# Two of eight remainder subtractions per phase moved from VectorE to GpSimd in the expert stage of a streaming encoder kernel

## The chip, the cores and the metric

One core of a Trainium2 chip. The time is the device time of one launch in microseconds, as the median of several runs.

## The reference

One layer of a streaming encoder runs on 512 prompt tokens and 128 sample tokens: a convolution branch and a gated delta-rule branch, merged by gates, then PEER expert retrieval, then a final norm. The change lies in the retrieval. Cut to what matters:

```python
def peer(xn, w_q, sub_keys, u, v):          # 16384 experts, 8 heads, top 16 of each
    ...                                     # idx, gate: (tokens, 8, 16)
    def block(args):
        xb, ib, gb = args
        hid = jnp.einsum('pd,phkd->phk', xb, u[ib])    # u, v: (16384, 2048)
        act = jax.nn.gelu(hid) * gb
        return jnp.einsum('phk,phkd->pd', act, v[ib])
```

## The kernel before

All is float32. There are five tiles of 128 tokens, and the expert stage treats them in two ways at once.

**Dense, tiles 0 to 2 (384 tokens).** TensorE multiplies the tokens with all 16384 rows of the first table `u`, GELU and a scattered gate follow, and the result is multiplied with the second table `v`. A float32 product is made of three passes with values cut in two: the high part (`xhi`, `whi`, `vhi`, `ahi`) and the remainder (`xlo`, `wlo`/`ulo`, `vlo`, `alo`). ScalarE makes each high part of a table's unit by a copy that rounds (`high`, `high_v`), and VectorE makes the remainder by a subtraction, raw minus high (`low` for the first table, L2857; `low_v` for the second, L2877). A unit is 128 x 1024 values, 512 KB.

**Gathered, tiles 3 and 4 (256 tokens).** Each token fetches only the rows of its 128 chosen experts. GpSimd asks for them by indirect DMAs of 128 rows of 2048 values (L2998): `u_rows` into two buffers `urow`, `v_rows` into two buffers `vrow`. VectorE takes a dot product with each row of `u` (`gather_dot`, L2899) and adds each row of `v` with its weight into the sum (`gather_add`, L2919). A request waits until the operation that used the row two numbers earlier is done, so that the two buffers alternate.

The stage runs in phases `c` = 1 to 32 with eight steps `j` = 0 to 7. Phases 2 to 31 are the full ones, 30 of them. The order on each engine is written out by hand. In a step of a full phase:

- TensorE: 24 matmuls of the first table (L2565, L2570), then it waits for the step's remainder `vlo`, then 18 matmuls of the second table (L2610 to L2612).
- ScalarE: `high` for the next step, `gelu_tile` in even steps, `high_v` for this step, `high_a` in odd steps from 3 on.
- VectorE: `low` for the next step, in even steps `gate` (L2867), `gather_dot`, `low_v` for this step, in odd steps from 3 on `low_a` (L2872), then `add_pair` (even, L2885, reads PSUM) or `add_third` (odd, L2893, reads PSUM), then `gather_add`.
- GpSimd: `u_rows`, then `v_rows`, and nothing else.
- SyncE and ScalarE's queue load the raw units.

The number of dots per step is one, with one exception that `dots` sets: in the phases 5, 10, 15, 20, 25 and 30 step 4 has two (I call these extra phases, the other 24 quiet ones):

```python
more = (c - 1) // 5 + (1 if c % 5 == 0 and j > NU // 2 else 0)
return min(FIRST_DOTS[NU] + (c - 2) * NU + j + more, GATHERS)
```

Of the kernel before, what the change touches and what calls it, by code (L numbers as in the profile page):

```python
# [85 lines left out]
def build(nc, x_prompt, x_sample, consts, params, conv_prefix, dconv_prefix, state_in, w_ba, w_first, w_units,  # L86
          keys, ffn_g, final_g, peer_u, peer_v, u_units, v_units,
          y_prompt, y_sample, conv_new_p, dconv_new_p, state_new_p, conv_new_s, dconv_new_s, state_new_s):
    with ExitStack() as ctx:
# [2228 lines left out]
        def sem2(name):  # L2318
            return ctx.enter_context(nc.semaphore(name))
# [86 lines left out]
        gt_ld = sem2("gt_ld")  # L2406
        hi_done, lo_done, unit_free, v_mm = (sem2(n) for n in ("hi_done", "lo_done", "unit_free", "v_mm"))
        gelu_done, a_done, v_add = (sem2(n) for n in ("gelu_done", "a_done", "v_add"))
        a_mul, a_hi, vhi_done, vlo_done = (sem2(n) for n in ("a_mul", "a_hi", "vhi_done", "vlo_done"))
        ggelu, gcoef, u_used, v_used = (sem2(n) for n in ("ggelu", "gcoef", "u_used", "v_used"))  # L2410
        u_ld = [sem2(f"u_ld{i}") for i in range(2)]
        v_ld = [sem2(f"v_ld{i}") for i in range(2)]
# [35 lines left out]
        def row_sums(c, j):  # L2448

            return 0 if c == 1 else (c - 2) * GRP + j if c < CHUNKS else TAIL + 2 * j  # L2450
        assert dots(CHUNKS - 1, NU) == dots(CHUNKS, 0) == GATHERS and row_sums(CHUNKS, NU) == GATHERS

        def phases(phase):

# [77 lines left out]
        def _(pe):  # L2532
# [50 lines left out]
            def phase(c, par, has_u):  # L2583
                for j in range(NU):
                    if has_u:
                        first_table(c * NU + j, j % 2, c * ET + j // 2, j // 2 % 2, lows=None if c == 1 else ulo[j % URING])
                    vh4, vl4 = (a.rearrange("p (e x) -> p e x", e=2) for a in (vhi[:, j % 2, :], vlo[j % VRING]))
                    v4 = vraw[j % VRING].rearrange("p (e x) -> p e x", e=2)
                    b, half = j // 2, j % 2
                    if has_u:  # L2590
                        pe.wait_ge(vlo_done, c * NU + (j + 1 - NU))
                    else:
                        pe.wait_ge(vn_ld[j % VRING], c * VLOADS + (16 * (j // VRING) + 16 - VLOADS))
                    for t in range(DT):
                        out = v_sum(b, t)
                        if half == 0 and t != 1:
                            pe.wait_ge(v_add, (c - 1) * NU + 2 * b + 1 + t // 2)
                        tok = slice(t * P, (t + 1) * P)
                        for q in range(2):
                            e = 2 * half + q  # L2600
                            first, last = half == 0 and q == 0, half == 1 and q == 1
                            if not has_u:
                                if b == 0 and t == 0:
                                    pe.wait_ge(a_hi, c * ET + (e + 1 - ET))
                                mmi = pe.matmul(out, aplain[1 - par][:, e, tok], v4[:, q, :], start=first, stop=last)
                                continue
                            if b == 0 and t == 0:
                                pe.wait_ge(a_done, c * ET + (e + 3 - ET))
                            a_h, a_l = ahi[1 - par][:, e, tok], alo[1 - par][e][:, tok]
                            pe.matmul(out, a_h, vh4[:, q, :], start=first, stop=False)  # L2610
                            pe.matmul(out, a_h, vl4[:, q, :], start=False, stop=False)  # L2611
                            mmi = pe.matmul(out, a_l, vh4[:, q, :], start=False, stop=last)  # L2612
                        if t:
                            mmi.then_inc(v_mm, 1)
# [136 lines left out]
        def _(v):  # L2751
# [177 lines left out]
            def phase(c, par, has_u):  # L2929
                first = is_first(c)  # L2930
                for j in range(NU):
                    if not has_u and j == 0:
                        v.wait_ge(v_used, CHUNKS // GT * GRP + 2)
                        v.sem_inc(f_ready, 1)
                    if not has_u and j == NU - 1:
                        v.wait_ge(f_gain, 16)
                        result(0)
                    if first:
                        low_v(j, j % 2, j % VRING)
                    if has_u and not (j == NU - 1 and is_last(c)):  # L2940
                        if first and j < NU - 1:
                            low_pre(NU + j + 1, (NU + j + 1) % PRE, (j + 1) % 2)
                        else:
                            low(c * NU + (j + 1), (j + 1) % 2, (j + 1) % URING)
                    if j == 0 and not first:
                        gate(c * ET - 1, ET - 1, 1 - par, c * 16 - 32)
                    if j == 0 and not first:
                        gather_coef(c - 2)
                    if j == NU // 2 and not has_u:
                        gather_coef(c - 1)  # L2950
                    if j and j % 2 == 0 and has_u:
                        e = j // 2 - 1
                        if e == 0:
                            wait_count(v, "dve", v_mm, c * KD + (4 - KD))
                        gate(c * ET + e, e, par, c * 16 - 16)
                    for n in range(dots(c, j), dots(c, j + 1)):
                        gather_dot(n)
                    if has_u and not first:
                        low_v(c * NU + (j - NU), j % 2, j % VRING)
                    if j == 0 and not first and has_u:  # L2960
                        low_a(c * ET - 1, ET - 1, 1 - par)
                    if j % 2 and j >= 3 and has_u:
                        e = (j - 3) // 2
                        if not is_last(c):
                            low_a(c * ET + e, e, par)
                    if first and j == 2:
                        v.wait_ge(f_ld, 16)
                    if j >= 2:
                        (add_third if j % 2 else add_pair)(c, j // 2 - 1)
                    elif not first:  # L2970
                        (add_third if j % 2 else add_pair)(c - 1, NU // 2 - 1)
                    if not has_u and j == NU - 1:
                        add_pair(c, NU // 2 - 1)
                        v.wait_ge(v_add, CHUNKS * NU + 3)
                        v.sem_inc(f_ready, 2)
                        add_third(c, NU // 2 - 1)
                        v.wait_ge(v_add, CHUNKS * NU + 4)
                        v.sem_inc(f_ready, 1)
                    for n in range(row_sums(c, j), row_sums(c, j + 1)):
                        gather_add(n)  # L2980
                if first:
                    v.wait_ge(x1g_ld, 16)
# [7 lines left out]
        @block2.gpsimd  # L2990
        def _(pool):
            pool.iota(iota_i2, pattern=[[1, NK]], base=0, channel_multiplier=0).then_inc(iota_ready, 1)
            pool.wait_ge(iota_ready, 1)
            pool.tensor_copy(iota_k[:], iota_i2).then_inc(iota_ready, 1)

            def rows(dst, table, n, ld):

                pool.indirect_dma_start(out=dst, out_offset=None, in_=table,  # L2998
                                        in_offset=bass.IndirectOffsetOnAxis(ap=gidx_all[:, n:n + 1], axis=0)).then_inc(ld, 16)

            def u_rows(n):

                if n == 0:
                    pool.wait_ge(oh_done, NQ)
                    pool.wait_ge(oh_key, NQ)
                elif n == 1:
                    pool.wait_ge(a_mul, ET)
                    pool.wait_ge(g_out[1], 16 * (NGG // 2))
                else:
                    pool.wait_ge(u_used, n + 1)  # L3010
                rows(urow[n % 2], peer_u, n, u_ld[n % 2])

            def v_rows(n):

                if n < TAIL + 2:
                    pool.wait_ge(v_used, n + 1)
                elif n < TAIL + 4:
                    pool.wait_ge(u_used, GATHERS + 2)
                else:
                    pool.wait_ge(v_used, n - 1)  # L3020
                if n < TAIL:
                    rows(vrow[n % 2], peer_v, n, v_ld[n % 2])
                else:
                    rows(tail_row[(n - TAIL) % 4], peer_v, n, tail_ld[(n - TAIL) % 4])

            def phase(c, par, has_u):
                for j in range(NU):
                    for n in range(dots(c, j), dots(c, j + 1)):
                        u_rows(n)
                    for n in range(row_sums(c, j), row_sums(c, j + 1)):  # L3030
                        v_rows(n)
            phases(phase)


# [93 lines left out]
```

## Time and profile before

| | |
|---|---|
| median of 3 runs | 4575.81 us (4572.33 to 4582.88) |
| the profiled execution | 4578.06 us, its span 4576.4 us, mean TensorE clock 0.983 |
| busy in the span | PE 97%, PEld 90%, DVE 75%, ACT 29%, POOL 29% |
| DVE in the second half of the slices | 9 tenths or more nearly throughout |
| DMA in the same slices | 9 tenths, 340 to 406 GB/s |
| L2899 (dots), DVE | 256, 2287 ns each, 585.1 us |
| L2919 (weighted adds), DVE | 256, 2348 ns each, 601.2 us |
| L2877 (`low_v`), DVE | 248, median 1222 ns |
| L2998 (row requests), POOL | 512, 1679 and 1519 ns each |

PE is TensorE's matmuls, PEld its weight loads, DVE VectorE, ACT ScalarE, POOL GpSimd. A share of the span is a mean over stages; the expert stage is the stretch from about 2410 to 4510 us.

### The profile page before, as it was taken

How to read it: one execution, taken by the hardware profiler on the slowest of the kernel's cores; microseconds unless marked ns; L12 is line 12 of the kernel's file. 1: busy time of each engine (PE TensorE's matmuls, PEld its weight loads, DVE VectorE, ACT ScalarE, POOL GpSimd, SP SyncE). 2: the span in 40 equal slices, each digit the busy share in tenths (PEclk: the TensorE clock that was granted, in tenths of full speed). 3: DMA queues.
4: the chain of work that ended last, by engine and by line, in shares of the span. 5: the costliest groups of instructions: out<-in, count | busy, mean ns of one | idle time of the engine just before them, and what ended most of it. 6: DMA issues, size and time to landing. Idle time of an engine off the chain costs nothing.

```text
span 4576.4 us, 67251 instructions
## 1 busy us (share of the span) xinstructions
PE 4426.4 (97%) x26165; PEld 4130.3 (90%) x26165; DVE 3443.6 (75%) x4196; ACT 1342.5 (29%) x1810; POOL 1348.8 (29%) x808
## 2 busy tenths in 40 slices
PE   7999999999999999999698999999999999999997
PEld 7999999999999998889687999989989989999995
DVE  4788884444443331058896999999999999999998
ACT  3323333222221211132282222222222222222222
POOL 0111123122222333323102343333344333343342
PEclk8999999999999999999899999999999999999999
DMA  3222223212224434231179999999999999999998
GB/s 114 88 85 88 84 91 100 75 61 75 79 84 159 136 120 156 87 124 65 58 222 357 391 387 406 389 380 392 388 386 396 394 374 393 389 391 396 394 390 340
DMA packets 255373, 1085.11 MB, mean 237 GB/s; under 512 B 23680, under 2 KB 72192, under 8 KB 181632
## 3 DMA queue, kind: packets, MB, share of 16 engines
q0 software_dynamic: 74752, 538.99, 30.1%
q1 hardware_dynamic: 140032, 400.12, 24.5%
q10 hardware_dynamic: 40320, 142.10, 8.0%
q8 instruction: 207, 3.39, 0.3%
q14 instruction: 62, 0.51, 0.0%
HBM read 1016.24 MB, written 64.88 MB: 236 GB/s over the span
## 4 chain that ended last, share of the span: by engine, by line
PE 44%; DVE 3%; DMA 2%; issue 1%; SPq 0%; ACT 0%; POOL 0%; DVEq 0%; ACTq 0%
PE ps L2565 14%; PE ps L2570 7%; PE ps L2610 7%; PE ps L2611 7%; PE ps L2612 7%; PE ps L2549 1%; DMA work<-in_peer_u,sel 1%; DMA work<-in_peer_v,sel 1%; DMA keep<-in_u_units 0%; DVE work L2899 0%; DVE work L2800 0%; DVE keep L2919 0%; SPq L2502 0%; DVE workr L2877 0%; DVE work L2802 0%
## 5 line engine op out<-in xcount | busy, mean ns | idle before, releaser
L487 PE MATMUL ps<-xhi,hi 128*128 128x320 f32 x2560 | 769.8, 314 | 16.0 <-ACTq L771 9.4
L487 PE MATMUL ps<-xlo,hi 128*128 128x320 f32 x2560 | 757.6, 309 | 0.0
L2565 PE MATMUL ps<-xhi,whi 128*128 128x384 f32 x2048 | 688.0, 336 | 0.0
L2565 PE MATMUL ps<-xlo,whi 128*128 128x384 f32 x2048 | 687.2, 336 | 0.0
L2998 POOL DMA_INDIRECT work<-in_peer_u,sel x256 | 429.9, 1679 | 799.9 <-DVE hid L2899 628.8
L2610 PE MATMUL ps<-vhi,ahi 128*128 128x512 f32 x1488 | 589.2, 396 | 22.9 <-DVE workr L2877 22.6
L2919 DVE SCALAR_TENSOR_TENSOR keep<-work,act_w,keep 128x2048 f32<-128x2048 f32 x256 | 601.2, 2348 | 6.4 <-DMA work<-in_peer_v,sel 5.8
L2899 DVE CUSTOM_DVE_ANT_0 work<-work,keep 128x2048 f32<-128x2048 f32 x256 | 585.1, 2287 | 19.4 <-DMA work<-in_peer_u,sel 18.1
L2611 PE MATMUL ps<-workr,ahi 128*128 128x512 f32 x1488 | 588.9, 396 | 0.0
L2998 POOL DMA_INDIRECT work<-in_peer_v,sel x256 | 388.8, 1519 | 671.0 <-DVE keep L2919 663.3
L2612 PE MATMUL ps<-vhi,alo 128*128 128x512 f32 x1308 | 516.2, 395 | 0.0
L487 PEld LDWEIGHTS ps<-xhi,hi 128*128 128x128 f32 x2560 | 481.7, 188 | 20.3 <-issue 11.6
L487 PEld LDWEIGHTS ps<-xlo,hi 128*128 128x128 f32 x2560 | 481.8, 188 | 2.2 <-issue 2.2
L487 PE MATMUL ps<-xhi,lo 128*128 128x320 f32 x2560 | 435.9, 311 | 0.0
L2565 PEld LDWEIGHTS ps<-xhi,whi 128*128 128x128 f32 x2048 | 384.6, 188 | 10.6
L2565 PEld LDWEIGHTS ps<-xlo,whi 128*128 128x128 f32 x2048 | 384.5, 188 | 10.1
L487 PEld LDWEIGHTS ps<-xhi,lo 128*128 128x128 f32 x2560 | 388.6, 188 | 1.4 <-issue 1.4
L1419 POOL TENSOR_TENSOR lo<-keep,hi 128x1024 fp32r<-128x1024 f32 x80 | 199.8, 2498 | 643.5 <-ACT hi L730 636.5
L2610 PEld LDWEIGHTS ps<-vhi,ahi 128*128 128x128 f32 x1488 | 281.5, 189 | 82.5 <-DVE workr L2877 27.1
L2676 ACT ACTIVATE whi<-work 128x1024 fp32r<-128x1024 f32 x120 | 127.4, 1061 | 723.6 <-PE ps L2570 723.6
L2676 ACT ACTIVATE whi<-wraw 128x1024 fp32r<-128x1024 f32 x120 | 127.4, 1061 | 694.0 <-PE ps L2570 687.7
L2611 PEld LDWEIGHTS ps<-workr,ahi 128*128 128x128 f32 x1488 | 281.3, 189 | 54.8
(349 smaller groups left out, 7806.2 us busy)
## 6 DMA issues: line engine op xcount, KB each, us to landing
work<-in_v_units ACTq DMA_DIRECT2D x256, 512.0 KB
keep<-in_w_first SPq DMA_DIRECT2D x160, 512.0 KB, 3.6
work<-in_u_units SPq DMA_DIRECT2D x120, 512.0 KB
wraw<-in_u_units SPq DMA_DIRECT2D x120, 512.0 KB
keep<-in_w_units SPq DMA_DIRECT2D x32, 1024.0 KB, 4.9
gates_dram<-work SPq DMA_DIRECT2D x8, 3072.0 KB, 11.8
gbuf<-gates_dram SPq DMA_DIRECT2D x30, 768.0 KB
arena<-in_w_units SPq DMA_DIRECT2D x32, 512.0 KB, 4.1
```

The lines of the kernel that those rows point to most:

```text
L487: m = pe.matmul(out[:, o:o + HT], w[:, k, :], x[:, 8 * kh + k, c], start=kh == 0 and i == 0, stop=kh == 1 and i == 23)
L1419: pool.tensor_tensor(lo_w(n), raw_w(n), hi_w(n).bitcast(F32), ALU.subtract).then_inc(lo_done, 1)
L2549: m = pe.matmul(ps[2 + r][:, b * P:(b + 1) * P], oneh[r][0][:, b, :], oneh[r][1][:, b, :], start=True, stop=True)
L2565: pe.matmul(out, h3[:, k, :], (xlo if m % 2 else xhi)[:, 8 * half + k, :], start=half == 0 and m == 0, stop=False)
L2570: mmi = pe.matmul(out, l3[:, k, :], xhi[:, 8 * half + k, :], start=False, stop=half == 1 and k == 7)
L2610: pe.matmul(out, a_h, vh4[:, q, :], start=first, stop=False)
L2611: pe.matmul(out, a_h, vl4[:, q, :], start=False, stop=False)
L2612: mmi = pe.matmul(out, a_l, vh4[:, q, :], start=False, stop=last)
L2676: act.activation(whi[:, r, :], uraw[slot], ACT.Copy).then_inc(hi_done, 1)
L2899: v.tensor_tensor_reduce(out=row, in0=row, in1=xg[:, n // SLOTS, :], scale=1.0, scalar=0.0, op0=ALU.mult, op1=ALU.add, accum_out=hid[:, h: ...
L2919: v.scalar_tensor_tensor(x1g[:, t, :], row, act_w2[:, j:j + 1], x1g[:, t, :], ALU.mult, ALU.add).then_inc(v_used, 1)
L2998: pool.indirect_dma_start(out=dst, out_offset=None, in_=table, in_offset=bass.IndirectOffsetOnAxis(ap=gidx_all[:, n:n + 1], axis=0)).then_ ...
```

## The change

In phases 2 to 31 the remainders of steps 2 and 5 are no longer made by VectorE. GpSimd makes them with the same subtraction, behind the row requests of the following step (3 and 6). It waits for ScalarE's high part and signals on a new semaphore `vlo_shared`; TensorE waits on that one in steps 2 and 5, and the count of VectorE's own remainders, `vector_lows`, is six a phase instead of eight. Phases 1 and 32 are as before. Nothing else changes; the subtraction gives the same values.

```diff
+        SHARED = (2, 5)
+
+        def vector_lows(c, j):
+
+            if c == 1:
+                return j + 1
+            return NU + (c - 2) * (NU - len(SHARED)) + j + 1 - sum(s <= j for s in SHARED)
...
                     if has_u:
-                        pe.wait_ge(vlo_done, c * NU + (j + 1 - NU))
+                        if c > 1 and j in SHARED:
+                            pe.wait_ge(vlo_shared, (c - 2) * len(SHARED) + SHARED.index(j) + 1)
+                        else:
+                            pe.wait_ge(vlo_done, vector_lows(c, j))
...
-                    if has_u and not first:
+                    if has_u and not first and j not in SHARED:
                         low_v(c * NU + (j - NU), j % 2, j % VRING)
...
+            def shared_low(n, r, slot):
+
+                pool.wait_ge(vhi_done, n + 1)
+                pool.tensor_tensor(vlo[slot], vraw[slot], vhi[:, r, :].bitcast(F32), ALU.subtract).then_inc(vlo_shared, 1)
...
                     for n in range(row_sums(c, j), row_sums(c, j + 1)):
                         v_rows(n)
+                    if has_u and c > 1 and j - 1 in SHARED:
+                        shared_low(c * NU + (j - 1 - NU), (j - 1) % 2, (j - 1) % VRING)
```

On VectorE, in step 5 of a full phase, before (ISA rows are the dot and the reading of its sum; L2877 is `low_v`, L2872 `low_a`, L2893 `add_third`, L2919 `gather_add`):

```order
L2857 TENSOR_TENSOR wlo<-wraw,whi 128x1024
L2899 ISA work,hid<-work,keep 128x2048
L2899 ISA hid 128x1
L2877 TENSOR_TENSOR workr<-work,vhi 128x1024
L2872 TENSOR_TENSOR alo0<-hbuf,ahi 128x384
L2893 TENSOR_TENSOR work<-work,ps3 128x512
L2919 SCALAR_TENSOR_TENSOR keep<-work,act_w2,keep 128x2048
```

The same step in the changed kernel, where line numbers are 11 higher:

```order
L2868 TENSOR_TENSOR wlo<-wraw,whi 128x1024
L2910 ISA work,hid<-work,keep 128x2048
L2910 ISA hid 128x1
L2883 TENSOR_TENSOR alo0<-hbuf,ahi 128x384
L2904 TENSOR_TENSOR work<-work,ps3 128x512
L2930 SCALAR_TENSOR_TENSOR keep<-work,act_w2,keep 128x2048
```

The subtraction between the dot and `low_a` is gone; step 2 loses it in the same way, between the dot and `add_pair`. On GpSimd, in the changed kernel, from the row requests of step 3 of a full phase to those of step 7:

```order
L3009 DMA work<-in_peer_u,sel 128x2048
L3009 DMA work<-in_peer_v,sel 128x2048
L3027 TENSOR_TENSOR workr<-work,vhi 128x1024
L3009 DMA work<-in_peer_u,sel 128x2048
L3009 DMA work<-in_peer_v,sel 128x2048
L3009 DMA work<-in_peer_u,sel 128x2048
L3009 DMA work<-in_peer_v,sel 128x2048
L3009 DMA work<-in_peer_u,sel 128x2048
L3009 DMA work<-in_peer_v,sel 128x2048
L3027 TENSOR_TENSOR workr<-work,vhi 128x1024
L3009 DMA work<-in_peer_u,sel 128x2048
L3009 DMA work<-in_peer_v,sel 128x2048
```

Before, this engine had the requests alone; now the subtraction of step 2 stands ahead of the requests of step 4, and that of step 5 ahead of those of step 7.

## Rows read from the trace of the kernel before

**Rows 1.** Windows: busy us of each engine (x instructions), granted clock, DMA, GB/s.

```profile
3500.00:3600.00 100.00, 100.00 (x505) 90.52 (x504) 97.81 (x86) 28.64 (x36) 37.14 (x24) 1.00 1.00 393
...
3070.00:3080.00 10.00, 6.97 (x29) 5.89 (x28) 7.26 (x7) 2.38 (x3) 1.94 (x3) 0.83 1.02 409
...
3750.00:3760.00 10.00, 10.00 (x39) 8.66 (x38) 10.00 (x9) 0.00 (x0) 3.55 (x3) 0.73 0.97 369
```

**Rows 2.** Waits of PE from 2500 to 4500 us: total, times, longest.

```profile
PE ps L2610 <- DVE workr L2877: 7.3, 7, 3.0
```

**Rows 3.** Timeline of DVE, step 2 of phase 17: start, us, what.

```profile
3515.48 2.29 DVE L2899 CUSTOM_DVE_ANT_0 work<-work,keep 128x2048 f32<-128x2048 f32 x1
...
3517.69 1.22 DVE L2877 TENSOR_TENSOR workr<-work,vhi 128x1024 fp32r<-128x1024 f32 x1
3518.83 1.21 DVE L2885 TENSOR_TENSOR work<-work,ps 128x1024 f32<-128x1024 f32 x1
3519.96 2.35 DVE L2919 SCALAR_TENSOR_TENSOR keep<-work,act_w,keep 128x2048 f32<-128x2048 f32 x1
```

**Rows 4.** Timeline of DVE, step 5 of phase 17.

```profile
3540.09 2.28 DVE L2899 CUSTOM_DVE_ANT_0 work<-work,keep 128x2048 f32<-128x2048 f32 x1
```

**Rows 5.** Timeline of POOL in the same phase.

```profile
3513.92 1.99 POOL L2998 DMA_INDIRECT work<-in_peer_v,sel  x1 [2.32 <-DVE keep L2919]
3518.04 1.68 POOL L2998 DMA_INDIRECT work<-in_peer_u,sel  x1 [2.13 <-DVE hid L2899]
...
3539.29 1.69 POOL L2998 DMA_INDIRECT work<-in_peer_v,sel  x1 [2.86 <-DVE keep L2919]
```

**Rows 6.** Timeline of PE: first second-table matmul of steps 2 and 5.

```profile
3520.88 0.39 PE L2610 MATMUL ps<-vhi,ahi 128*128 128x512 f32 x1
...
3545.96 0.39 PE L2610 MATMUL ps<-vhi,ahi 128*128 128x512 f32 x1
```

**Rows 7.** Earlier stages, timeline: DVE and POOL where they overlap.

```profile
810.45 2.40 POOL L1419 TENSOR_TENSOR lo<-keep,hi 128x1024 fp32r<-128x1024 f32 x1 [10.13 <-ACT hi L730]
...
811.99 1.21 DVE L1289 TENSOR_TENSOR arena<-arena,ps 128x1024 f32<-128x1024 f32 x1
...
1466.12 1.22 DVE L1348 TENSOR_TENSOR arena<-arena,smalld 128x1024 f32<-128x1024 f32 x1
...
1466.38 3.19 POOL L1419 TENSOR_TENSOR lo<-keep,hi 128x1024 fp32r<-128x1024 f32 x1 [9.25 <-ACT hi L730]
...
817.71 2.42 POOL L1419 TENSOR_TENSOR lo<-keep,hi 128x1024 fp32r<-128x1024 f32 x1 [4.86 <-ACT hi L730]
...
817.79 2.88 DVE L1302 TENSOR_TENSOR arena<-cst,keep 128x512 f32<-128x512 f32 x1
```

**Rows 8.** Lines of the source: count, ns min/median/max, first and last start.

```profile
L1302 DVE TENSOR_TENSOR arena<-cst,keep x10: 678/685/2889, 817.8 to 1351.3; 128x512 f32<-128x512 f32 x10
...
L1227 DVE SCALAR_TENSOR_TENSOR arena<-arena,par x232: 1117/1134/3284, 141.1 to 708.1; 128x880 f32<-128x880 f32 x116
```

**Rows 9.** Timeline of phase 10, steps 5 and 6 (DVE, POOL, PE).

```profile
3072.74 2.29 DVE L2899 CUSTOM_DVE_ANT_0 work<-work,keep 128x2048 f32<-128x2048 f32 x1 [3.63 <-DMA work<-in_peer_u,sel]
...
3081.03 2.29 DVE L2899 CUSTOM_DVE_ANT_0 work<-work,keep 128x2048 f32<-128x2048 f32 x1
...
3069.10 0.94 POOL L2998 DMA_INDIRECT work<-in_peer_v,sel  x1 [0.30 <-issue]
...
3076.24 0.80 PE L2610 MATMUL ps<-vhi,ahi 128*128 128x512 f32 x1 [3.03 <-DVE workr L2877]
...
3086.21 0.39 PE L2610 MATMUL ps<-vhi,ahi 128*128 128x512 f32 x1
```

**Rows 10.** Timeline of phase 5, step 5 (DVE, PE).

```profile
2737.42 1.23 DVE L2877 TENSOR_TENSOR workr<-work,vhi 128x1024 fp32r<-128x1024 f32 x1
...
2739.32 0.39 PE L2610 MATMUL ps<-vhi,ahi 128*128 128x512 f32 x1
```

**Rows 11.** Chain that ended last, 3055 to 3090 us: start, us, what.

```profile
3061.51 11.21 DMA work<-in_peer_u,sel
```

More of the change, by code:

```diff
@@ L2408, in build @@
         gelu_done, a_done, v_add = (sem2(n) for n in ("gelu_done", "a_done", "v_add"))
-        a_mul, a_hi, vhi_done, vlo_done = (sem2(n) for n in ("a_mul", "a_hi", "vhi_done", "vlo_done"))
+        a_mul, a_hi, vhi_done, vlo_done, vlo_shared = (sem2(n) for n in ("a_mul", "a_hi", "vhi_done", "vlo_done", "vlo_shared"))
         ggelu, gcoef, u_used, v_used = (sem2(n) for n in ("ggelu", "gcoef", "u_used", "v_used"))
```

## Prediction

> **What bounds the kernel now.** I read the windows first. In a quiet stretch of the expert stage PE is busy for 100.00 of 100 us at the full clock, DVE for 97.81, POOL for 37.14, and the DMA share is 1.00 [rows 1]. So TensorE sets the pace there, VectorE has 2.19% left, and the DMA queues have next to nothing left. The reader is to see three engines at their limit at once: work taken off VectorE is worth only what TensorE waits for it. The list of waits gives that: from 2500 to 4500 us TensorE waits 7.3 us in all for `low_v`, seven times, at most 3.0 us [rows 2]. The timelines show where. In a quiet phase `low_v` is ready well ahead: in step 2 it ends at 3517.69 + 1.22 = 3518.91 and TensorE comes at 3520.88, in step 5 it ends at 3543.52 (the dot's start 3540.09, the 2.21 from a dot's start to the next operation's, and 1.22) and TensorE comes at 3545.96 [rows 3, 4, 6]. The gaps are 1.97 and 2.44 us. The 7.3 us lie in the extra phases, most of them in phases 10 and 20. In phase 10 the dot of step 5 waits 3.63 us for its row, then `low_v` follows, and TensorE waits 3.03 us [rows 9]. TensorE's clock falls after that wait: the window 3070 to 3080 has a granted clock of 0.83 (between the levels 2.4 and 1.2 GHz), and after the like wait of phase 20 the window 3750 to 3760 has 0.73 [rows 1]. Those two windows cost 10 x 0.17 = 1.7 and 10 x 0.27 = 2.7 us more.
>
> The profiled execution took 4578.06 us, 2.25 above the median of 4575.81, with 1.7 of it outside its span. The terms below are differences and go onto either.
>
> **VectorE's account, quiet phase.** Removed: two subtractions. From the start of one to that of the next operation it is 3518.83 - 3517.69 = 1.14 us [rows 3], so 2.28 us a phase. Added on GpSimd: two subtractions of the same form as L1419, 2.42 us where it runs at once [rows 7], 4.9 us a phase on an engine that is 37% busy. If they were free for the others, VectorE would gain 2.28 us a phase.
>
> They are not free. Where GpSimd's subtraction and a VectorE operation that reads two tiles of SBUF meet, one waits for the other. At 1466.12 VectorE was first: its 1.22 us are not lengthened, and GpSimd's operation took 3.19. At 817.71 GpSimd was first: VectorE's L1302 took 2.88 us [rows 7] against a median of 0.685, 2.20 more, and L1227 goes from a median of 1.134 to 3.284, 2.15 more [rows 8]. An operation that reads one tile of SBUF and one of PSUM is not touched: L1289 takes 1.21 us at 811.99, inside POOL's subtraction of 810.45 to 812.85 [rows 7]. The Trainium skill, "SBUF — State Buffer", section "Who interferes with whom", has this as a rule: the shared pair of ports goes to whoever issues first, for the whole instruction, the other fully blocks, and a VectorE instruction with two SBUF inputs contends with GpSimd's reads. The trace agrees.
>
> *Step 2.* GpSimd comes to the subtraction after the request of 3513.92, which ended at 3515.91; with about 0.3 us of issue that is 3516.2, inside the dot that runs 3515.48 to 3517.77 [rows 3, 5]. It is granted at the dot's end and VectorE is locked out for 2.15 us from 3517.69, until 3519.84. `add_pair` reads PSUM and runs 3517.69 to 3518.83 beside it. `gather_add` then starts at 3519.84 instead of 3519.96 [rows 3]. Net: -0.12 us.
>
> *Step 5.* The request of 3539.29 ends at 3540.98, the subtraction is asked for at 3541.3, inside the dot of 3540.09 to 3542.37 [rows 4, 5]. What follows the dot is `low_a`, with two SBUF inputs: it is blocked for 2.15 us from 3542.30, where 1.14 were saved. Net: +1.01 us.
>
> So VectorE's load rises by 0.89 us a phase. It has 2.19% of 66.7 us (a step is (3545.96 - 3520.88) / 3 = 8.36 us [rows 6], a phase 66.7) = 1.46 left, and keeps 0.57. Over five phases, with the extra dot (3517.69 - 3515.48 = 2.21 us), 7.3 - 2.2 = 5.1 us were free, and 0.6 remain. That is just enough, and the mechanism decides at a load of 5.1 / 5 = 1.02 us a phase.
>
> **TensorE's waits, quiet phases.** GpSimd's result comes about 2.3 us after the dot's end: 3520.05 in step 2, TensorE at 3520.88; 3544.65 in step 5, TensorE at 3545.96 [rows 3, 4, 6]. The slack shrinks to 0.8 and 1.3 us, no wait. Cost 0. The cover that hides it is TensorE's own work; if GpSimd took 0.8 us longer, each step 2 would cost.
>
> **The row requests behind.** The request of 3518.04 now stands behind the subtraction (3520.3). A request is itself held by a running two-input VectorE operation: that of 3518.04 ends 0.8 us after `low_v`'s end of 3518.91 [rows 3, 5]. Now it meets `gather_add` (until 3522.2) and ends near 3523.0 instead of 3519.72, 3.3 us later. The dot that uses its row comes two steps on, 16.7 - 2.2 = 14.5 us after the old issue; the slow landing shown took 11.21 us [rows 11]. Margin 3.3, delay 3.3: mostly covered, in phases behind an extra one not. I put 1 us in all, bounds 0 and 6.
>
> **Extra phases 10 and 20.** GpSimd reaches the subtraction of step 5 after the request of 3069.10 + 0.94, at 3070.3, while VectorE stands idle until 3072.74 [rows 9]. It is done by 3072.8, before TensorE is ready at 3076.24 - 3.03 = 3073.21. That wait goes. Step 6 of TensorE would then be ready at 3081.5, but its `low_v` follows a dot that can start only 1.14 us earlier than 3081.03 [rows 9]; it ends at 3079.9 + 2.2 + 1.2 = 3083.4. So a wait of 1.9 us is late next, and TensorE starts step 6 at 3083.4 instead of 3086.21: -2.8 us, or -1.1 if the clock falls again for 1.7. I take -2 for each: -4.
>
> **Extra phases 5, 15, 25, 30.** In phase 5 `low_v` was released by the dot at 2737.42 and TensorE came at 2739.32 [rows 10]. Granted at the dot's end (2737.50), GpSimd delivers at 2739.8: a new wait of 0.5. Four times: +2.
>
> **Recovery.** After an extra phase VectorE is late by up to its 2.2 us dot and now catches up by 0.57 a phase instead of 1.46. In step 2 of the five phases behind one GpSimd's result is 1.1 us later than `low_v` was. I put 0.5 for each, +2.5, bounds 0 and 5.6.
>
> **Sum.** 1 - 4 + 2 + 2.5 = +1.5, rounded to +2: 4578 on the median (4580 in the profiled execution's terms). About 0.2%, 9.2 us, is what a measurement here can tell from no change. With the bounds of the terms (-1.1 to -2.8 for each of phases 10 and 20) the sum runs from -4 to +12.
>
> **Rivals.**
> 1. *Slower: VectorE becomes the bound.* If GpSimd comes to step 2's subtraction before the dot (it was 0.7 us behind its start, 3516.2 against 3515.48), the dot is blocked whole, 2.2 - 1.14 = 1.06 us instead of -0.12. With step 5 that is 2.1 us a phase against 1.46 free: 0.66 x 30 = 20 us, and the six extra dots are no longer hidden, 13 us, less the 7.3 us of waits that they already cause: +26, 4602. The break-even load is 1.02 us and I forecast 0.89, so that 0.15 us more in each GpSimd subtraction already costs (0.30 - 0.13) x 30 = 5 us. For it: that narrow margin, VectorE's 97.81%, DMA at 1.00. Against: the request before it is itself held by the subtraction `low`, which keeps it behind the dot's start. Chance 0.34. The Trainium skill, "Perfetto Trace Analysis", section "Optimizing Scalar/DVE Operations", says that moving work between VectorE and GpSimd might not help, since they share a read port; here that would take the form of this rival.
> 2. *Faster: the waits of TensorE go and nothing comes back.* At most the 7.3 us with the clock's 1.7 + 2.7, 12 us: 4564. For it: in phases 10 and 20 the subtraction falls into idle time. Against: [rows 7, 8]. Chance 0.08.
>
> **Chances and range.** The forecast, within 4567 to 4585, has 0.58; slower by over 0.2% 0.34, faster 0.08. The range of eight in ten reaches from 4570 to rival 1's 4602. The likeliest case's own range is 4570 to 4588.
>
> **What the profile after would show.** The subtraction on POOL 60 times, 3.8 us each in step 2 and 3.3 in step 5, since it waits inside for the dot. `low_a` with a maximum near 2.7 us instead of 0.55, in the 30 steps 5; `gather_add` in step 2 near 3.4 us instead of 2.35. `low_v` 188 times. DVE near 98.9 to 99% in the quiet window, PE still at 100. The 3.03 us wait of phase 10 gone, with one of about 2 us in its step 6. PE waiting for POOL in steps 5 of the extra phases. Wrong would make it: dots that are lengthened to 4.4 us in step 2 (rival 1), VectorE operations with two SBUF inputs that keep their length beside GpSimd's (rival 2), or TensorE waiting in the quiet phases.

## The result and the profile after

The changed kernel takes 4610.71 us (median of 4 runs, 4607.92 to 4615.74) against 4574.07 us of the kernel before, measured beside it (4570.01 to 4582.88). The ratio is 1.008, interval 1.0067 to 1.0093. It is 36.6 us slower, and outside the range of the prediction. The profiled execution took 4607.92 us with a span of 4606.3, against 4578.06 and 4576.4 before: 29.9 us more. In all readings of the profile after, line numbers are 11 higher than before: the dot is L2910, `low_v` L2888, `low_a` L2883, `gather_add` L2930, and GpSimd's subtraction L3027.

From the page: busy time, the chain that ended last, and the group of the dot (busy us, mean ns of one, idle before it and what ended most of that).

```profile
PE 4439.5 (96%) x26165; PEld 4128.5 (90%) x26165; DVE 3509.0 (76%) x4136; ACT 1342.6 (29%) x1810; POOL 1496.6 (32%) x868
...
DVE 33%; issue 12%; DMA 3%; PE 3%; SPq 0%; ACT 0%; POOL 0%; DVEq 0%; ACTq 0%
...
L2910 DVE CUSTOM_DVE_ANT_0 work<-work,keep 128x2048 f32<-128x2048 f32 x256 | 675.2, 2639 | 19.0 <-DMA work<-in_peer_u,sel 17.9
```

VectorE lost 60 subtractions, yet its busy time rose. A dot takes 2639 ns in the mean where it took 2287. The chain that ended last holds 33% of VectorE and 3% of TensorE; in the kernel before it held 3% and 44%.

The windows after, first the quiet one that answers to [rows 1], then phases 3 to 30 whole (from TensorE's first second-table matmul of phase 3 to that of phase 31):

```profile
3500.00:3600.00 100.00, 99.76 (x500) 89.63 (x500) 99.93 (x83) 29.26 (x38) 46.49 (x27) 1.00 0.99 389
...
2562.30:4474.14 1911.84, 1886.53 (x9410) 1692.58 (x9410) 1900.49 (x1553) 544.43 (x700) 880.67 (x510) 1.00 0.98 385
```

The same 28 phases of the kernel before:

```profile
2563.75:4444.79 1881.04, 1873.50 (x9410) 1694.73 (x9409) 1836.70 (x1608) 544.39 (x700) 737.15 (x454) 1.00 0.99 390
```

VectorE's work grew from 1836.70 to 1900.49 us: 63.8 us, or 2.28 a phase. Its idle time fell from 44.3 to 11.4 us, so 33.0 us of the growth went into idle time, and the other 30.8 came onto the stage, which is 1911.84 - 1881.04 = 30.8 us longer, the 29.9 of the span within a microsecond. Such a split comes out for any engine, since busy and idle time add up to the window. What makes VectorE the bound is how little of it is left idle. The same windows phase by phase, over the 22 quiet ones among these 28: VectorE was idle for 1.37 us in the mean before and for 0.03 to 0.04 us in each of them after; a quiet phase grew by 0.81 us, 17.9 in all. The six extra phases together grew by 12.9, from 414.4 to 427.3. The granted clock of both windows is 1.00, so the loss is not the clock's.

Where the growth sits, the timelines show. Step 2 of phase 17, POOL and then DVE:

```profile
3528.12 1.69 POOL L3009 DMA_INDIRECT work<-in_peer_v,sel  x1 [2.32 <-DVE keep L2930]
3529.83 2.41 POOL L3027 TENSOR_TENSOR workr<-work,vhi 128x1024 fp32r<-128x1024 f32 x1
```

```profile
3529.38 5.02 DVE L2910 CUSTOM_DVE_ANT_0 work<-work,keep 128x2048 f32<-128x2048 f32 x1
...
3534.33 1.21 DVE L2896 TENSOR_TENSOR work<-work,ps 128x1024 f32<-128x1024 f32 x1
```

GpSimd's subtraction begins 0.02 us after its request ends and takes the 2.41 us of an unhindered one. The dot is recorded as starting 0.45 us ahead of it, and still it takes 5.02 us instead of 2.29 [rows 3]: it is the dot that waited, 2.73 us. This is so in 29 of the 30 steps 2; in the first of them GpSimd starts 0.23 us ahead of the dot, which takes 4.48. Step 5 of the same phase:

```profile
3555.93 3.61 POOL L3027 TENSOR_TENSOR workr<-work,vhi 128x1024 fp32r<-128x1024 f32 x1
```

```profile
3555.02 2.28 DVE L2910 CUSTOM_DVE_ANT_0 work<-work,keep 128x2048 f32<-128x2048 f32 x1
...
3557.23 2.73 DVE L2883 TENSOR_TENSOR alo<-hbuf,ahi 128x384 fp32r<-128x384 f32 x1
```

Here the dot starts 0.91 us ahead and keeps its 2.28; GpSimd waits inside (3.61), and `low_a` then takes 2.73 instead of 0.55. By the single operations a full phase has 2.73 - 1.14 = +1.59 us in step 2 and 2.18 - 1.14 = +1.04 in step 5, 2.63 together. The windows' 2.28 is less mainly because a `gather_add` with idle time behind it counts 2.35 us, and one that the next operation follows at once 2.26 up to that operation's start. In phase 17 four had idle time behind them before and none has after: 0.36 us, which leaves 2.27. In the steps 5 of the extra phases one dot (3.4 to 4.5 us) bears the conflict.

TensorE's waits from 2500 to 4530 us (total, times, longest), which were 7.3 us for one line before [rows 2]:

```profile
PEld ps L2621 <- DVE workr L2888: 29.4, 39, 2.4
PE ps L2621 <- DVE workr L2888: 18.1, 10, 2.1
PEld ps L2621 <- POOL workr L3027: 14.0, 22, 0.8
...
PE ps L2621 <- POOL workr L3027: 6.9, 21, 0.4
```

PE and PEld wait beside each other, so the rows don't add up. There are many short waits, most for VectorE's `low_v`, some for GpSimd's result: VectorE is late everywhere. A quiet phase takes 67.2 to 67.8 us instead of 66.45 or 66.88, by TensorE's first second-table matmuls; the extra phases 5, 15, 25 and 30 take 71.2, 71.2, 71.1 and 72.5 instead of 67.3, 68.2, 67.3 and 66.9; phases 10 and 20 got shorter, 70.6 and 70.8 instead of 71.8 and 72.9.

### The profile page after: what moved, and what is told of

It is laid out like the page before. It is cut to its first block, busy times and chain, and to the rows that moved or that the text cites. A ratio compares the mean times of both kernels' runs of the same rounds, so it can differ in the third digit from the quotient of the medians.

```text
span 4606.3 us, 67251 instructions
## 1 busy us (share of the span) xinstructions
PE 4439.5 (96%) x26165; PEld 4128.5 (90%) x26165; DVE 3509.0 (76%) x4136; ACT 1342.6 (29%) x1810; POOL 1496.6 (32%) x868
## 4 chain that ended last, share of the span: by engine, by line
DVE 33%; issue 12%; DMA 3%; PE 3%; SPq 0%; ACT 0%; POOL 0%; DVEq 0%; ACTq 0%
DVE work L2910 12%; DVE keep L2930 7%; DVE workr L2888 4%; DVE work L2896 3%; DVE alo L2883 2%; DMA work<-in_peer_u,sel 2%; DVE work L2904 2%; PE ps L2557 1%; DVE hbuf L2878 1%; DMA work<-in_peer_v,sel 1%; DVE wlo L2868 1%; PE ps L2573 1%; DVE workr L2868 1%; DMA keep<-in_u_units 0%; DVE work L2811 0%
## 5 line engine op out<-in xcount | busy, mean ns | idle before, releaser
L2910 DVE CUSTOM_DVE_ANT_0 work<-work,keep 128x2048 f32<-128x2048 f32 x256 | 675.2, 2639 | 19.0 <-DMA work<-in_peer_u,sel 17.9
L3009 POOL DMA_INDIRECT work<-in_peer_v,sel x256 | 414.9, 1621 | 652.8 <-DVE keep L2930 646.7
L3009 POOL DMA_INDIRECT work<-in_peer_u,sel x256 | 384.2, 1501 | 693.9 <-DVE hid L2910 519.4
L2930 DVE SCALAR_TENSOR_TENSOR keep<-work,act_w,keep 128x2048 f32<-128x2048 f32 x256 | 600.8, 2347 | 8.1 <-DMA work<-in_peer_v,sel 7.4
```

What stands on the lines that cost most here:

```text
L2910: v.tensor_tensor_reduce(out=row, in0=row, in1=xg[:, n // SLOTS, :], scale=1.0, scalar=0.0, op0=ALU.mult, op1=ALU.add, accum_out=hid[:, h: ...
L2930: v.scalar_tensor_tensor(x1g[:, t, :], row, act_w2[:, j:j + 1], x1g[:, t, :], ALU.mult, ALU.add).then_inc(v_used, 1)
```

## The experiments

The names in the expectations: A is the theory that VectorE's load is the cause and that in step 2 the dot is blocked whole; B puts the loss elsewhere (TensorE waiting for GpSimd's late results, or requests standing behind the subtractions). Each edit is against the changed kernel. Where a memset is added the dot is L2911 and the subtraction L3030 to L3032.

**Each half alone.**

```diff
-        SHARED = (2, 5)
+        SHARED = (2,)
```

> GpSimd makes the remainder of step 2 alone; step 5 is VectorE's again. Theory A (load): in the changed kernel's trace the dot of step 2 takes 5.01 us instead of 2.28, so VectorE loses 2.73 and saves 1.14, +1.59 us a phase, against 1.02 us that it has free on the mean of five phases. 0.57 x 30 = 17 us more than before: 4591 (4586 to 4596). Theory B (late results): TensorE waits for GpSimd's result and for late rows, and that happens in step 5 (the waits for POOL lie there); without it the time is before's within 4 us, 4570 to 4578. The dot is long in 30 steps 2 by either theory.

Measured: 4581.16 us (4578.10 to 4584.15) against 4576.27, ratio 1.0009, interval 1.0 to 1.0019.

```diff
-        SHARED = (2, 5)
+        SHARED = (5,)
```

> GpSimd makes the remainder of step 5 alone. Theory A: the dot keeps its 2.28 us, the alo subtraction behind it takes 2.73 instead of 0.55, so VectorE loses 2.18 and saves 1.14, +1.04 us a phase against 1.02 free on the mean: between 0 and +6 us, 4574 to 4580. Theory B: most of the 36 us stay, above 4595.

Measured: 4579.02 us (4572.19 to 4583.02), ratio 1.0001, interval 0.9991 to 1.0011.

In the first, the dots' maximum is 5.021 us, as in the changed kernel; in the second `low_a` reaches 2.750. In the window 3500 to 3600 VectorE is busy for 99.90 us with step 2 alone and for 98.85 with step 5 alone, and TensorE stays at 100.00 in both.

Neither half costs anything like half of 36.6 us: step 2 alone adds 4.9 us, step 5 alone at most 5. That is how a threshold looks, and step 5 alone speaks for A and against B, whose cost for it was about 20 us or more. But step 2 alone lies in neither range: A, with a break-even load of 1.02 us a phase, expected 4586 to 4596, B 4570 to 4578. The trace shows where the threshold lies. By the windows of its 22 quiet phases VectorE's busy time is 1.38 us a phase above that of the kernel before, which had 1.37 us idle; 0.05 us are left idle, and the phase is 66.72 us long instead of 66.67. So step 2 alone fills VectorE just to the brim.

**The two remainders by nobody.** In phases 2 to 31 the remainders of steps 2 and 5 are left out, and the second pass of their products takes the high part again, so the output is not the reference's. This is the upper bound of what any helper could give.

```diff
-                            pe.wait_ge(vlo_shared, (c - 2) * len(SHARED) + SHARED.index(j) + 1)
+                            pe.wait_ge(vhi_done, c * NU + (j + 1 - NU))
+                            vl4 = vh4
...
-                    if has_u and c > 1 and j - 1 in SHARED:
-                        shared_low(c * NU + (j - 1 - NU), (j - 1) % 2, (j - 1) % VRING)
```

> The two remainders are left out of the computation: nobody makes them, and the pass over the remainder in steps 2 and 5 uses the high part again, so TensorE's work is the same. This is what the removal from VectorE alone is worth. Both theories: VectorE's load falls by 2.28 us a phase, the waits of TensorE of 7.3 us and the clock's loss of up to 4.4 us behind them go for the most part: -5 to -11 us, 4563 to 4569. If it were -20 or more, TensorE would not be the bound of the stage before.

Measured: 4572.02 us (4569.21 to 4579.46) against 4576.27, ratio 0.9984, interval 0.9974 to 0.9994. That is 4 us faster than before by the medians and 7 by the ratio, and above the 4563 to 4569 expected. VectorE falls to 94.62 of 100 us. All there was to win is about 0.1 to 0.2%.

**Who comes first in step 2.** Two memsets of 240 columns on GpSimd, each waited for, stand ahead of step 2's subtraction.

```diff
+        pause, paused = sb2("pause", [P, 240]), sem2("paused")
...
+                if r == 0:
+                    for k in range(2):
+                        pool.memset(pause[:], 0.0).then_inc(paused, 1)
+                        pool.wait_ge(paused, (n // NU) * 2 + k - 1)
                 pool.wait_ge(vhi_done, n + 1)
```

> As the changed kernel, but in step 2 GpSimd first does two small memsets one after the other (about 0.3 us each), so that its subtraction is asked for about 1 us after the dot's start instead of 0.45. Theory A with order of arrival as the cause of the long dot: the dot of step 2 keeps 2.28 us, GpSimd's subtraction takes 3.4 to 3.8 us, the weighted add of step 2 takes about 3.4; VectorE's load is +0.9 instead of +2.63 us a phase, and the time is 4576 to 4586. Theory A with the dot losing whatever the order: dot 5.0 us, 4610. Theory B: the result comes later than now, so 4610 or more.

Measured: 4581.01 us (4577.04 to 4584.80), ratio 1.001, interval 1.0001 to 1.002. GpSimd does more, yet the kernel is some 30 us faster than the changed one. In 29 of the 30 steps 2 the dot starts 1.18 us ahead of the subtraction and keeps 2.28, and `gather_add` takes 3.35. The first case is of another kind; POOL and DVE in step 2 of phase 2:

```profile
2513.74 4.05 POOL L3032 TENSOR_TENSOR workr<-work,vhi 128x1024 fp32r<-128x1024 f32 x1
```

```profile
2513.26 2.29 DVE L2911 CUSTOM_DVE_ANT_0 work<-work,keep 128x2048 f32<-128x2048 f32 x1
```

The dot is only 0.48 us ahead and wins. In the changed kernel it was 0.45 ahead and lost. And in step 5 of phase 15 of this same kernel, where GpSimd comes straight from a request, it is 0.59 ahead and loses:

```profile
3413.50 2.41 POOL L3032 TENSOR_TENSOR workr<-work,vhi 128x1024 fp32r<-128x1024 f32 x1
```

```profile
3412.91 5.16 DVE L2911 CUSTOM_DVE_ANT_0 work<-work,keep 128x2048 f32<-128x2048 f32 x1 [0.24 <-DMA work<-in_peer_u,sel]
```

So no single bound on the recorded lead decides. The next pair tests why: C says that a subtraction right behind a request takes the shared reads before its recorded start, D that any small delay on GpSimd is enough.

**A one-column memset without and with a wait.** `pause` has one column here. First without:

```diff
+                if r == 0:
+                    pool.memset(pause[:], 0.0).then_inc(paused, 1)
                 pool.wait_ge(vhi_done, n + 1)
```

> As the changed kernel, with one memset of a single column on GpSimd ahead of the subtraction of step 2, and no wait between them. Theory C (early claim): the subtraction claims the shared read interface while the row request ahead of it is still being finished, so before its recorded start; that is how the dot loses though it is recorded 0.45 us earlier. A memset that waits for nobody lets the claim through: the dot of step 2 stays near 5.0 us, load +2.6 us a phase, 4600 to 4612. Theory D (a dot claims late, some 0.5 us after its recorded start, since it is a custom operation): a delay of 0.1 to 0.2 us is enough, the dot keeps 2.28 and the time is 4577 to 4586.

Measured: 4610.52 us (4609.04 to 4611.17) against 4574.64, ratio 1.0077, interval 1.0061 to 1.0094. Then the same memset, waited for:

```diff
+                if r == 0:
+                    pool.memset(pause[:], 0.0).then_inc(paused, 1)
+                    pool.wait_ge(paused, n // NU)
                 pool.wait_ge(vhi_done, n + 1)
```

> The same with a wait for that memset ahead of the subtraction, so that the subtraction can't begin before everything ahead of it on GpSimd is complete. Theory C: the dot keeps its 2.28 us, the subtraction takes 3.7 to 4.1 us, 4577 to 4586. Theory D: as e5, the dot 2.28 us as well if the delay reaches 0.5 us after the dot's start, otherwise 5.0. C and D are told apart by e5 together with this one: they differ in C and are alike in D.

Measured: 4580.36 us (4578.99 to 4586.50), ratio 1.0016, interval 1.0007 to 1.0026. The one wait is worth 30 us. The timelines of a step 2, without the wait:

```profile
3532.83 0.11 POOL L3029 MEMSET pause<- 128x1 f32 x1
3532.88 2.41 POOL L3030 TENSOR_TENSOR workr<-work,vhi 128x1024 fp32r<-128x1024 f32 x1
```

```profile
3532.39 5.06 DVE L2911 CUSTOM_DVE_ANT_0 work<-work,keep 128x2048 f32<-128x2048 f32 x1
```

and with it:

```profile
3517.27 0.11 POOL L3029 MEMSET pause<- 128x1 f32 x1
3517.46 3.91 POOL L3031 TENSOR_TENSOR workr<-work,vhi 128x1024 fp32r<-128x1024 f32 x1
```

```profile
3516.83 2.28 DVE L2911 CUSTOM_DVE_ANT_0 work<-work,keep 128x2048 f32<-128x2048 f32 x1
...
3520.17 3.35 DVE L2931 SCALAR_TENSOR_TENSOR keep<-work,act_w,keep 128x2048 f32<-128x2048 f32 x1
```

Without the wait the dot is 0.49 us ahead (0.47 to 0.49 in nearly all steps) and loses. With a wait it won at a lead of 0.48 in the run before this, and wins here at 0.62. In all the traces together a dot beside a subtraction that comes straight from a request loses at recorded leads up to 0.60 us and wins from 0.69 on, with none in between. At equal leads the wait decides, so recorded starts alone don't. C holds, D falls.

The length of a beaten dot says the same. A dot longer than 2.5 us occurs 118 times in the traces of all runs, each time beside a subtraction, and it ends 2.15 to 2.16 us after the subtraction's end, whether it is recorded as starting 0.60 us ahead of the subtraction or 1.5 us behind. What it is recorded as running before GpSimd's start brings it nothing.

The second timeline is step 2 as the prediction had it: the dot keeps its length, and GpSimd's turn falls beside `add_pair`. `gather_add` is then 1.01 us longer where 1.14 was saved, -0.13 us net; the prediction said -0.12. And the kernel takes 4580, where it said 4578. GpSimd makes the same two remainders a phase here and ends that of step 2 4.54 us after the dot's start, where the changed kernel takes 2.86; so late results, theory B, aren't the cause.

The Trainium skill, "GPSIMD Engine Reference", section "Instruction dispatch", warns that GpSimd's cores do not run in lockstep: each goes on to the next instruction once its own share of the one before is done. That would make such an early claim possible. The trace shows the claim and what removes it, not the single cores, so this reading is not shown.

**Is it the shared reads?** GpSimd writes zeros instead of the difference, so it reads nothing. The remainders of these two steps are then zero: this kernel leaves their part of the product out.

```diff
-                pool.tensor_tensor(vlo[slot], vraw[slot], vhi[:, r, :].bitcast(F32), ALU.subtract).then_inc(vlo_shared, 1)
+                pool.memset(vlo[slot].bitcast(F32), 0.0).then_inc(vlo_shared, 1)
```

> GpSimd writes zeros in place of each of the two remainders, at the same places and with the same waits: the subtraction is left out of the computation, and GpSimd reads nothing from SBUF there. If it is the shared read interface that blocks VectorE, the dot of step 2 keeps 2.28 us and the alo subtraction of step 5 0.55, and the time is that of e3 within 4 us, 4567 to 4575. If any work of GpSimd there does it (its write, or its late requests), both stay lengthened and the time stays above 4590.

Measured: 4574.85 us (4568.63 to 4580.80), ratio 0.9998, interval 0.9988 to 1.0007. Its lines of the source for the dot and `low_a` (count, ns min/median/max):

```profile
L2910 DVE CUSTOM_DVE_ANT_0 work<-work,keep x256: 2281/2285/2361, 2429.4 to 4490.2; 128x2048 f32<-128x2048 f32 x128
```

```profile
L2883 DVE TENSOR_TENSOR alo<-hbuf,ahi x105: 547/553/559, 2449.1 to 4437.8; 128x384 fp32r<-128x384 f32 x105
```

Same order, same waits, same writes into the same buffer: no dot is above 2.36 us and no `low_a` above 0.56. The memset starts 0.43 us behind the dot of step 2, where the subtraction started 0.45 behind, and runs beside it for all of its 0.97 us without either getting longer. So the blocking of the dot goes with the two operands that GpSimd reads. In step 5 the memset is done before the dot ends, and `low_a` doesn't meet it: there the run shows that the loss goes with the subtraction, and not whether a write of the same length would block `low_a`.

**Another step.**

```diff
-        SHARED = (2, 5)
+        SHARED = (1, 5)
```

> GpSimd makes the remainders of steps 1 and 5 instead of 2 and 5. Step 1 has no gate ahead of its dot, so the dot should win there as in step 5; behind it stands the third add, 0.60 us and reading PSUM, and then the weighted add, which is held: 2.18 - 0.60 - 1.14 = +0.44. With step 5's +1.04 the load grows by 1.48 us a phase. The mean phase of the kernel before is 67.2 us with its stalls, VectorE's work 65.2 and 0.44 for the extra dots, so 1.57 are free. Theory A: 4574 to 4582, and 25 to 35 us faster than the changed kernel with the same number of subtractions moved. If the number of subtractions on GpSimd is what counts, 4605 or more.

Measured: 4584.90 us (4581.99 to 4589.73), ratio 1.0021, interval 1.0011 to 1.0031. The same number of remainders, 25.8 us faster than the changed kernel: the rival by which the mere number moved decides (4605 or more) falls. The remainder of step 1 falls beside VectorE's step 1, an odd one with no `gate` ahead of the dot, so the dot starts 0.92 us before the subtraction and keeps its 2.28, and `gather_add` takes 3.88. The load is 3.88 - 2.35 - 1.14 = +0.39 and +1.04, 1.43 a phase; by the windows of the quiet phases 1.34, just under the 1.37 free. It came out 3 us above what was expected; with so little free, single phases (the one behind each extra phase takes 67.1 to 67.8 instead of 66.45 or 66.88) already pay.

**Only where VectorE stands idle.** The remainder of step 5 in phases 10 and 20 goes to GpSimd, nothing else.

```diff
+        def is_shared(c, j):
+
+            return c in (10, 20) and j == 5
...
```

> GpSimd makes one remainder only, that of step 5 in phases 10 and 20, where VectorE stood idle for 3.63 us (phase 10) waiting for rows; everywhere else as before. Theory (what a phase gains or loses is set by VectorE's free time in it, and the gain of phases 10 and 20 seen in e2_only5, 68.57 and 68.71 against 71.76 and 72.85 us, is the removed instruction and the wait behind it): 4 to 7 us less than before, 4567 to 4571 against 4574. Rival (those phases end with the rows' arrival, and what is saved there is handed back in the next phases, or the gain came of the lighter phases around): within 2 us of before, 4572 to 4576.

Measured: 4575.14 us (12 runs, 4570.92 to 4587.47) against 4576.88, ratio 0.9996, interval 0.9986 to 1.0006. The rival's range, not mine. In its profile phases 10 and 20 are shorter, 69.4 and 68.6 us for 71.8 and 72.9, though their dots are blocked too (5.00 and 4.66 us, leads 0.42 and 0.11). But phases 5, 15 and 30, in which nothing was changed, take 71.5, 72.2 and 73.1 us where they took 67.3, 68.2 and 66.9. This execution took 4587.47 us, the slowest of the 12, so its trace can't say whether the gain of phases 10 and 20 is handed back or only lost in the scatter of the extra phases. That stays open.

The loads side by side. The middle columns are the means of the 22 quiet phases in each kernel's one profiled execution: what VectorE's busy time grew by, what it has left idle (1.37 us before), and how long the phase is (66.67 us before).

| kernel | load by single operations, us a phase | VectorE busy | idle left | phase, us | ratio to before |
|---|---|---|---|---|---|
| step 5 alone | +1.04 | +0.85 | 0.52 | 66.67 | 1.0001 |
| two memsets, each waited for | -0.13 + 1.04 = +0.91 | +0.88 | 0.55 | 66.72 | 1.0010 |
| memset and wait | -0.13 + 1.04 = +0.91 | +0.91 | 0.51 | 66.72 | 1.0016 |
| steps 1 and 5 | +0.39 + 1.04 = +1.43 | +1.34 | 0.20 | 66.84 | 1.0021 |
| step 2 alone | +1.59 | +1.38 | 0.05 | 66.72 | 1.0009 |
| memset, no wait | +1.64 + 1.04 = +2.68 | +2.12 | 0.04 | 67.46 | 1.0077 |
| changed kernel | +1.59 + 1.04 = +2.63 | +2.15 | 0.04 | 67.48 | 1.0080 |

Up to the idle time of a quiet phase the ratio stays within 1.0021, and beyond it the kernel is 0.8% slower. Below it the order of the ratios is not that of the loads. In the traces the 28 phases take 1881.30 us with the memset and the wait and 1878.44 with step 2 alone, against 1881.04 before, so neither shows its 0.16 or 0.09% there; steps 1 and 5 take 1885.21, 4.2 us more than before, 3.7 of them in the five phases behind an extra one. One execution of each kernel can't tell more.

## Why the prediction was wrong

**The bound now: right.** TensorE sets the pace, and VectorE's work beyond it is worth little: leaving the two remainders out altogether gives 4 to 7 us.

**Step 2: the step that failed.** "with about 0.3 us of issue that is 3516.2, inside the dot ... Net: -0.12 us" is wrong in both parts. There is no 0.3 us of issue: the subtraction is recorded 0.02 us after the request's end. And it is not the recorded start that decides: at 0.45 us behind the dot's start GpSimd still went first. The dot was blocked whole and lengthened by 2.73 us, net +1.59 instead of -0.12. The kernel with the memset and the wait, where the dot does go first, shows that this one step of the account is the difference between 4580 and 4611.

**Step 5: right.** Net +1.01 was predicted and +1.04 measured, `low_a` at 2.73 with 2.7 predicted. The subtraction takes 3.6 us where 3.3 was forecast.

**VectorE's free time: mis-sized.** I reckoned 1.02 us a phase on the mean of five. The experiments put the threshold of a quiet phase at its idle time, 1.37 us in the mean: loads of 1.34 and 1.38 lengthen it by 0.17 and 0.06 us, one of 2.15 by 0.81. The window of all 28 phases gives 44.3 / 28 = 1.58, but 9.9 us of it lie in phases 10 and 20, where VectorE waits for rows and TensorE waits too. By itself this left the forecast more room than it claimed.

**TensorE's waits in quiet phases: wrong in the outcome.** No wait was forecast for GpSimd's results in a quiet phase. In phases 16 to 19 TensorE waits 0.24 to 0.41 us in each step 5. It goes with step 2, where VectorE becomes late: with the memset and the wait TensorE waits for GpSimd 4 times in the stage, in the changed kernel 21 times.

**The row requests behind: nothing.** From 2500 us on the dots wait 8.5 us for rows, where they waited 8.6; 1 us was forecast.

**Extra phases.** The wait of 3.03 us in phase 10 is gone from step 5, as forecast. But a wait of 1.93 us for `low_v` now stands in step 4, behind the extra dot, and the granted clock of 3070 to 3080 is 0.83 as before. Phases 10 and 20 gained 1.2 and 2.1 us with all of the change in (-2 each was predicted). The four others lost 3.0 to 5.6 us each, where +0.5 was forecast: VectorE has nothing left when the extra dot comes. Nor is there any catching up behind them at 0.57 us a phase, as the term for the recovery had it.

**Rivals.** Rival 1 named the mechanism, the dot of step 2 blocked whole and VectorE the bound, and got a chance of 0.34. Its price of +26 was too small, and its own numbers give a little less: (1.06 + 1.01 - 1.46) x 30 = 18 us for the quiet part, not 20. Its 1.06 us for step 2 should have been 1.59, because I took the 2.2 us of an operation that starts right behind GpSimd's for one that had started already. Its 1.46 free was near the 1.37 measured. It had 0.66 us for each of 30 phases where a quiet one grew by 0.81, and 0.66 x 6 + 13 - 7.3 = 9.7 us for the extra phases, where they grew by 12.9. The reason against it was that the dot starts first. That reason was true of the recorded starts and did not help. Rival 2 has nothing for it.

## What to carry to other kernels

Before work moves from VectorE to GpSimd, list the two-input SBUF operations of VectorE that it will meet, and price each meeting at the blocked operation's added time: here the subtraction saved 1.14 us and cost 2.18 or 2.73. A margin of half a microsecond by recorded starts is no margin when GpSimd's operation stands right behind another one on its queue; a semaphore wait ahead of it made a difference of 30 us here. And take an engine's free time phase by phase, and don't count idle time in which the engine that sets the pace waits too: here a mean over the stage said 1.58 us where a quiet phase had 1.37, and 1.38 already filled it.

## What was unexpected in the hardware

GpSimd's subtraction wins over a dot that is recorded as starting up to 0.60 us earlier when it stands right behind a row request, and up to 0.49 us earlier behind a one-column memset that is not waited for. Behind a request the dot wins from a lead of 0.69 us on; with a semaphore wait on the memset it wins at leads of 0.48 and 0.62 us. The loser's time then grows: up to 5.16 us for a dot of 2.28, 3.91 or 4.05 for a subtraction of 2.41. A beaten dot ends 2.15 to 2.16 us after GpSimd's operation, whatever its recorded lead, so that it is lengthened by more than one operation of GpSimd lasts (2.73 against 2.41 us); `low_a`, which begins when the turn passes, by 2.18. A memset of GpSimd that runs for 0.97 us beside a dot lengthens nothing.
